# Stick-breaking attention: causal mask as a table on VectorE instead of mask products on TensorE, and softplus in four ScalarE passes

## The reference, cut to what matters

```python
z = jnp.einsum('bqhd,bkhd->bhqk', q, k).astype(jnp.float32) * (HEAD_DIM ** -0.5)
z = z + b_sb.astype(jnp.float32)[None, :, None, None]
mask = k_pos[None, :] < q_pos[:, None]
log_keep = jnp.where(mask, jax.nn.log_sigmoid(-z), 0.0)
after = lax.cumsum(log_keep, axis=3, reverse=True) - log_keep
a = jnp.where(mask, jnp.exp(jax.nn.log_sigmoid(z) + after), 0.0)
return jnp.einsum('bhqk,bkhd->bqhd', a.astype(v.dtype), v)
```

## Time and profile before

| | |
|---|---|
| median of three runs | 875.83 us (872.63, 875.83, 875.88) |
| the profiled execution's own time | 872.5 us |
| its span in the trace | 870.7 us |
| PE busy | 825.4 us |
| DVE, ACT, POOL busy | 526.9, 348.9, 376.9 us |
| granted TensorE clock, mean | 0.989 |

### The profile page before, as it was taken

The page is one execution under the profiler, slowest core; times in us unless marked ns, Lnnn a source line. Parts: engine busy times, 40 slices in busy tenths (PEclk is TensorE's granted clock), DMA queues, the critical chain, the costliest instruction groups (busy, mean ns, idle before and its releaser), DMA issues.

```text
span 870.7 us, 15500 instructions
## 1 busy us (share of the span) xinstructions
PE 825.4 (95%) x4267; PEld 488.4 (56%) x4267; DVE 526.9 (61%) x691; ACT 348.9 (40%) x682; POOL 376.9 (43%) x186
## 2 busy tenths in 40 slices
PE   0899989999999999999999999999999999899996
PEld 0455756555667565565765655658555555344442
DVE  2554678676584767737857768287686774223334
ACT  6311057574112575811136666211565741111222
POOL 0006782653677355525865455268446430100000
PEclk9989999999999999999999999999999999999998
DMA  8997685576788866657888675687986757373101
GB/s 320 331 309 254 219 268 168 170 226 207 234 253 270 276 208 215 222 172 252 270 271 261 223 244 177 200 256 252 282 249 212 238 185 302 106 236 100 71 24 51
DMA packets 129221, 191.25 MB, mean 220 GB/s; under 512 B 9817, under 2 KB 50822, under 8 KB 129121
## 3 DMA queue, kind: packets, MB, share of 16 engines
q1 hardware_dynamic: 97920, 174.38, 60.9%
q10 hardware_dynamic: 31200, 15.73, 6.4%
HBM read 181.58 MB, written 8.51 MB: 218 GB/s over the span
## 4 chain that ended last, share of the span: by engine, by line
PE 88%; DVE 3%; issue 2%; SPq 2%; DMA 2%; ACT 1%; POOL 1%; POOLq 0%; DVEq 0%; ACTq 0%
PE ps L1144 83%; PE ps L1300 4%; DMA pages<-in_page_table_dram 1%; PE ps L1185 1%; SPq L319 1%; POOL prod L539 1%; DMA hT<-in_w_out_dram 1%; DVE xy L851 1%; DVE ps L1024 0%; DMA ring<-in_cache_v_dram 0%; PE ps L1327 0%; SPq L359 0%; SPq L351 0%; DVE zc L1030 0%; ACT gcb L572 0%
## 5 line engine op out<-in xcount | busy, mean ns | idle before, releaser
L1144 PE MATMUL ps<-hT,wsl 128*128 128x344 f32 x1344 | 425.3, 458 | 3.5 <-issue 3.5
L539 POOL TENSOR_TENSOR prod<-ring,qb 128x1024 f32<-128x1024 f32 x128 | 313.2, 2470 | 220.3 <-DMA ring<-in_cache_k_dram 93.9
L1144 PEld LDWEIGHTS ps<-hT,wsl 128*128 128x128 f32 x1344 | 241.6, 190 | 156.7 <-issue 43.0
L1000 DVE TENSOR_REDUCE zd<-prod 128x16 f32<-128x1024 f32 x128 | 154.1, 1213 | 37.1 <-POOL prod L539 35.9
L1010 DVE TENSOR_SCALAR zc<-ps,bsb 128x512 f32<-128x512 f32 (+3 forms) x96 | 55.5, 613 | 70.3 <-PE ps L1144 68.9
L1144 PE MATMUL ps<-ring,apad 128*8 128x512 f32 (+1 forms) x608 | 82.9, 626 | 2.5 <-DMA ring<-in_cache_v_dram 2.2
L572 ACT ACTIVATE av<-ps 128x512 f32<-128x512 f32 (+3 forms) x96 | 46.7, 487 | 86.2 <-PE ps L1300 85.4
L1144 PE MATMUL ps<-hT,xy 128*128 128x512 f32 x160 | 72.1, 594 | 0.5 <-DMA hT<-in_w_out_dram 0.5
L1024 DVE TENSOR_TENSOR_SCAN ps<-rise,ps 128x512 f32<-128x512 f32 (+3 forms) x64 | 65.6, 1025 | 9.8 <-ACT ps L572 8.7
L1144 PEld LDWEIGHTS ps<-wsl,hT 128*128 128x128 f32 (+1 forms) x576 | 63.5, 181 | 6.2 <-ACT vN L572 2.6
L1144 PE MATMUL ps<-wsl,hT 128*128 128x128 f32 (+1 forms) x576 | 66.5, 275 | 0.0
(11 more groups left out here) (210 smaller groups left out, 662.6 us busy)
## 6 DMA issues: line engine op xcount, KB each, us to landing
ring<-in_cache_k_dram SPq DMA_DIRECT2D x256, 256.0 KB, 3.0
ring<-in_cache_v_dram SPq DMA_DIRECT2D x256, 256.0 KB, 3.0
wsl<-in_w_in_dram ACTq DMA_DIRECT2D x30, 512.0 KB, 5.7
ring<-in_w_ada_dram SPq DMA_DIRECT2D x6, 2048.0 KB, 11.3
xy<-in_x_prompt_dram SPq DMA_DIRECT2D x2, 2048.0 KB, 10.4
out_dram<-oT SPq DMA_DIRECT2D x8, 512.0 KB, 4.0
ring<-in_x_prompt_dram SPq DMA_DIRECT2D x8, 512.0 KB, 6.5
hT<-in_w_out_dram SPq DMA_DIRECT2D x5, 512.0 KB, 5.6
```

What stands on the lines that cost most here:

```text
L539: pool.tensor_tensor(prod[:, p % 2].rearrange("p (j c) -> p j c", j=2), kring[:, p % 4], qb[:, p // 16].unsqueeze(1).to_broadcast([P, 2, H ...
L1000: v.tensor_reduce(zd[:, t // 16, :, r:r + 2], prod[:, t % 2].rearrange("p (j h d) -> p h j d", j=2, h=NH), AX_X, ALU.add)\
L1144: return nc.tensor.matmul(out, l, r, start=start, stop=stop, skip_group_check=True)
```

## The change

The mask moves from PE to DVE. A table `seen` (128 x 512, float32) is made once: in its last 128 columns it holds -2^100 where key is not before query and +2^100 elsewhere. The clamp of a diagonal unit becomes minimum(z + bias, table); that of the others adds the bias alone. The clamp at 40 is gone, so softplus is made as relu(zc) + ln(1 + exp(-abs(zc))), in four ACT passes: Abs, Exp, Ln, Relu. The scan reads `rise` unshifted, and the carry is a copy.

```diff
-            pool.memset(unseen[:, :], HIDE).then_inc(pool_const, 1)
-            pool.memset(ident_b[:, :], 0.0).then_inc(pool_const, 1)
+            pool.memset(seen[:, :], HIDE).then_inc(pool_const, 1)
...
+            pool.affine_select(out=seen[:, :], in_=seen[:, :], compare_op=ALU.is_ge, fill=-HIDE, base=P - QC,
+                               pattern=[[1, QC]], channel_multiplier=-1).then_inc(pool_const, 1)
...
-                        run(rise[:, u % 2, lo:QC], ps[:, Z + u % 3, 0:QC - lo], ACT.Relu, rise_ready,
-                            bias=bsh[:, bass.ds(2 * g + head, 1)])
                         z = sp[:, u % 2, lo:QC]
-                        run(z, zc[:, u % 3, lo:QC], ACT.Exp, exp_done)
+                        run(z, zc[:, u % 3, lo:QC], ACT.Abs, abs_done)
+                        act.wait_ge(abs_done, NU * g + u + 1)
+                        run(z, z, ACT.Exp, exp_done, scale=-1.0)
                         act.wait_ge(exp_done, NU * g + u + 1)
                         run(ps[:, Z + u % 3, 0:QC - lo], z, ACT.Ln, ln_done, bias=1.0)
+                        run(rise[:, u % 2, lo:QC], zc[:, u % 3, lo:QC], ACT.Relu, rise_ready)
...
-                v.tensor_scalar(zc[:, u % 3, lo:QC], ps[:, Z + u % 3, 0:QC - lo],
-                                bsb[:, bass.ds(2 * g + h, 1)], CLAMP, ALU.add, ALU.min).then_inc(zc_ready, 1)
+                t, b0, nb, _ = UNITS[u]
+                bias = bsb[:, bass.ds(2 * g + h, 1)]
+                if b0 + nb - 1 == t:
+                    v.scalar_tensor_tensor(zc[:, u % 3, lo:QC], ps[:, Z + u % 3, 0:QC - lo], bias, seen[:, lo:QC],
+                                           ALU.add, ALU.min).then_inc(zc_ready, 1)
+                else:
+                    v.tensor_scalar(zc[:, u % 3, lo:QC], ps[:, Z + u % 3, 0:QC - lo], bias, None, ALU.add)\
+                        .then_inc(zc_ready, 1)
...
-                v.tensor_tensor_scan(back(sums), back(rise[:, par_, lo + 1:QC + 1]), back(sums),
+                v.tensor_tensor_scan(back(sums), back(rise[:, par_, lo:QC]), back(sums),
                                      start, ALU.add, ALU.add).then_inc(scan_done, 1)
...
-                    v.tensor_scalar(carry[:, h:h + 1], sums[:, 0:1], rise[:, par_, 0:1], None, ALU.add)\
+                    v.tensor_copy(carry[:, h:h + 1], sums[:, 0:1])\
                         .then_inc(carry_ready, 1)
...
-                    diagonal = b0 + nb - 1 == t
-                    if diagonal:
-                        for h in range(2):
-                            mm(ps[:, Z + (u + h) % 3, P * (nb - 1):P * nb], unseen[:, :], ident_b[:, :], True, False)
                     for h in range(2):
                         rows_ = slice(HD * h, HD * (h + 1))
-                        z = mm(ps[:, Z + (u + h) % 3, 0:P * nb], qT[rows_, P * t:P * (t + 1)],
-                               kT[rows_, P * b0:P * (b0 + nb)], not diagonal, True)
-                        z.then_inc(z_full, 1)
+                        mm(ps[:, Z + (u + h) % 3, 0:P * nb], qT[rows_, P * t:P * (t + 1)],
+                           kT[rows_, P * b0:P * (b0 + nb)], True, True).then_inc(z_full, 1)
```

More of the change, by code:

```diff
@@ L48 @@
 EPS = 1e-6
-CLAMP = 40.0
 HIDE = -2.0 ** 100
@@ L57 @@
 SAMPLE_AT = OUT_UNITS - 3
-POOL_CONSTS = 9
+POOL_CONSTS = 7
 SLOTS = 32
@@ L140, in stick_breaking_mixer @@
         zc = sb("zc", [P, 3, QC])
-        rise = sb("rise", [P, 2, QC + 1])
+        rise = sb("rise", [P, 2, QC])
         carry = sb("carry", [P, 2])
-        bsh = sb("bsh", [P, NH])
         last2 = sb("last2", [P, 2])
@@ L163, in stick_breaking_mixer @@
         nones = sb("nones", [P, P], F32R)
-        unseen = sb("unseen", [P, P], BF16)
-        ident_b = sb("ident_b", [P, P], BF16)
+        seen = sb("seen", [P, QC])
         ones = sb("ones", [P, P])
@@ L213, in stick_breaking_mixer @@
         q_out = sem("q_out"); q_full = [sem(f"q_full{k}") for k in range(2)]
-        z_full = sem("z_full"); zc_ready = sem("zc_ready"); exp_done = sem("exp_done")
+        z_full = sem("z_full"); zc_ready = sem("zc_ready"); abs_done = sem("abs_done"); exp_done = sem("exp_done")
         ln_done = sem("ln_done"); rise_ready = sem("rise_ready")
@@ L487, in _ @@
             pool.memset(half[:, :], -0.5).then_inc(pool_const, 1)
-            pool.memset(unseen[:, :], HIDE).then_inc(pool_const, 1)
-            pool.memset(ident_b[:, :], 0.0).then_inc(pool_const, 1)
-            pool.wait_ge(pool_const, 5)
+            pool.memset(seen[:, :], HIDE).then_inc(pool_const, 1)
+            pool.wait_ge(pool_const, 4)
             pool.affine_select(out=ident[:, :], in_=ident[:, :], compare_op=ALU.not_equal, fill=1.0, base=0,
@@ L820, in _ @@
             v.memset(keep[:, :, :], 1.0).then_inc(dve_const, 1)
-            v.memset(rise[:, :, QC:QC + 1], 0.0).then_inc(dve_const, 1)
             v.memset(naught[:, :], 0.0).then_inc(dve_const, 1)
-            v.wait_ge(dve_const, 9)
+            v.wait_ge(dve_const, 8)
             v.memset(keep[:, :, 0:1], 0.0).then_inc(dve_const, 1)
@@ L829, in _ @@
             v.tensor_copy(nones[:, :], minus1).then_inc(dve_const, 1)
-            v.wait_ge(dve_const, 13)
+            v.wait_ge(dve_const, 12)
             v.wait_ge(c_act, 3)
@@ L875, in _ @@
                                     ALU.mult, ALU.add).then_inc(h_ready, 1)
-            link(v.tensor_scalar(bsh[:, :], bsb[:, :], -CLAMP, None, ALU.add))
             PRO = links[0]
@@ L1156, in _ @@
             last.then_inc(par_full, 1)
-            pe.wait_ge(dve_const, 13)
+            pe.wait_ge(dve_const, 12)
             pe.wait_ge(cT_copied, 1)
```

## The result

The changed kernel takes **877.17 us** (median of 11 runs, 876.12 to 879.40). The kernel before, run beside it, takes 874.74 us (11 runs, 872.48 to 875.88). The ratio is 1.0034 [1.0022, 1.0046]: 2.4 to 3 us slower, where 6.8 us were forecast. The direction was right, the size was not. 877.2 lies inside the recorded range of 875.5 to 888, near its lower end, and within 0.5% of before, an outcome that had a chance of 0.21.

The account below looks back on a forecast made before the run. PE was taken as the bound, busy 95% of the span, other engines costing only when late for it. Masks -3.6 us plus turn waits 10.4 gave +6.8 on 875.83, 882.6 us; range 875.5 to 888 for 8 in 10.

Parts of the forecast that it names:

- Masks off PE, 3.6 us: Ahead of the 32 diagonal score pairs, removing 64 mask products saves PE 0.112 us a pair, 3.6 us.
- The table clamp, the carry copy, POOL's set-up: On DVE and POOL, the clamp reading a table (751 ns against 747), the copy and the set-up cost nothing.
- rival D: On DVE, the table clamp fights POOL for SBUF, taking about 1.26 us for 512 columns; about 893 us, chance 0.04.
- The passes, +0.59 us a wide unit with the scan behind relu: On ACT, four passes take 2.44 us instead of 1.83 in a unit of 512 columns, with relu last.
- the seven turns: PE's transposes of units 6, 8, 12, 16, 18, 20, 22 in each group, forecast to wait for the longer chain.
- The mean of the seven is 0.20, so the reserve is 0.20 - 0.05 = 0.15: At seven turns a group, 0.15 us is free from subtraction end to weight load, so 7 x (0.59 - 0.15) = 3.1 us.
- That the narrow units 0, 2, 4, 10 and 14 would not wait: In groups 2 to 4 their turns feel nothing: the reserve exceeds their pass or DVE is late anyway.
- the forecast's 10.4 us: Added PE waits at the turns of all four groups, 3.1 + 3.1 + 4.2 us; bounds 6.2 and 12.4.
- B, the other side: At the turns, the chain has unseen room, so only the masks count: 872.2 us, chance 0.12.
- C: ACT's queue becomes the bound and av delays the next score pair too; about 890 us, chance 0.08.
- E: TensorE's clock falls to its lower level in places of the attention stretches; about 916 us, chance 0.02.
- The base: The time of the kernel before that the sum was added to: median of three runs, 875.83 us.

Follow-up runs that it names:

- numbers4_after: The changed kernel with SyncE reading four page numbers at once where two pairs follow each other; 874.69 us, ratio 0.9999 to before.
- numbers4_before: The kernel before with SyncE reading four page numbers at once where two pairs follow each other; 872.67 us, ratio 0.9977.
- The fifth pass: The kernel before with softplus in four passes and a plain-addition clamp, masks kept on PE, plus an ACT copy ahead of Relu; 895.45 us, ratio 1.0224.
- the pair with the shorter reading of page numbers: The kernel before and the changed kernel, each with SyncE reading four page numbers at once; 872.67 and 874.69 us.
- numbers4_masks: The kernel before with the table clamp, no mask products and three passes, plus SyncE reading four page numbers at once; 871.02 us, ratio 0.9952.
- masks_only: The kernel before with the table in DVE's clamp and no mask products, its three passes kept; 872.03 us, ratio 0.9969.
- passes_only: The kernel before with softplus in four passes and the clamp a plain addition, mask products kept on PE; 881.09 us, ratio 1.0072.
- before_again: The kernel before, unchanged, executed once more for a second trace; 875.44 us, span 873.7.
- turn_later: The changed kernel with one more projection product ahead of the turns of even units; 874.27 us, ratio to before 1.0005.

## Why the prediction was right in direction and wrong in size

**Masks off PE, 3.6 us: right.** 28 pairs give 0.112 us each. The four that open a group give 0.421 - 0.203 = 0.218, which I had set equal to the others: 4.0 us, or 63 ns for a mask. The 81 ns of the Trainium skill ("TensorE: Matmul & The Clock Gate", section Back-to-back issue gap) would be 5.2 us. The traces differ from it both ways, 56 ns a mask inside a group and 109 at the four openings, and their sum decides for 4.0.

**The table clamp, the carry copy, POOL's set-up: right.** 746 ns; rival D is refuted.

**The passes, +0.59 us a wide unit with the scan behind relu: right.** By unit 16's rows 2.47 us against 2.44; the chain from score to subtraction grew by 0.63 us as the mean of the seven turns (slack used and wait added), where 0.59 was forecast.

**"The mean of the seven is 0.20, so the reserve is 0.20 - 0.05 = 0.15": this step failed.** I took the reserve from the subtraction's end to the weight load. What PE needs is the matmul, and the load stands 0.29 us ahead of it. By starts of matmuls, unit 16 of group 2 had 344.88 - 344.31 = 0.57 us, unit 18 had 0.24 and not 0.05. Less the 0.06 at which a waiting matmul follows the subtraction, the seven have 3.0 us in hand in group 2 as in group 3, 0.42 each, and 3.4 in groups 1 and 4. So 7 x 0.63 - 3.0 = 1.4 us a group, and 1.0 in group 4. With the queue out of the way (numbers4_after less numbers4_before) the traces show 1.5, 1.5 and 1.0 in groups 2, 3 and 4, and 1.7 in group 1, at its units 2, 6 and 8: 5.7 us together instead of 10.4. A row of the prediction said so already: unit 18's load already waited 0.20 us, and yet PE was busy 101.0 of 101 us. The fifth pass, with nothing left in hand, cost what the formula says.

With that term corrected, and in the pair with the shorter reading of page numbers, where no scan waits for decode keys, the sum is -4.0 + 5.7 = +1.7 us, or +2.9 with the 1.2 us of the late second matmuls (22 more). The medians differ by 874.69 - 872.67 = +2.0. In the runs of the change itself they differ by +2.4. The agreement is of the total alone: the halves both fall short. numbers4_masks gains 1.7 us on numbers4_before where the sum has 4.0, and numbers4_after loses 3.7 on numbers4_masks where it has 5.8 to 7.0. With 12 runs each such a difference is good to about 1.7 us.

The recorded range has two figures that no run shows: the masks at 5.2 us, in its lower end, where the traces give 4.0, and at 2, in its upper end.

**That the narrow units 0, 2, 4, 10 and 14 would not wait, "or DVE is late anyway": incomplete.** In the pair of traces units 2, 4 and 8 of groups 3 and 4 carry 4.7 us of waits, 4.4 beyond what unit 8 waits in group 2; the first trace of before has none. They make the 10.9 us of that pair look like the forecast's 10.4. They are not the passes': masks_only has them too, passes_only has not, and the second trace of before has 2.5 us of them. Nor are they all extra time, for the seams are shorter where they occur: by 2.7 us in the changed kernel, 1.7 in masks_only and 1.6 in before_again, against waits of 4.4, 4.0 and 2.5 us. As I read it, not shown by a run of its own, the decode stream (SyncE's queue, then POOL, then DVE) keeps its own pace through the seam, and how PE's lateness divides between seam and unit 2 differs from run to run. My view of one execution had all of it at the seam.

**B, the other side, was the nearer rival**: its mechanism (a reserve unseen at the load) was the true one, with 0.42 us a turn, less than a pass of 0.63. For the masks to win it would have needed 0.63 - 0.14 = 0.49 or more, since 4.0 us over 28 turns are 0.14 each. C did not occur in the changed kernel. Its sign, score pairs that wait behind av, appears in turn_later, where the turn and not ACT's queue makes av late. E occurred in a small form, and not through the change: inside attention and at the seams products at half clock appear behind some waits of PE of 1.7 us and more, with the kernel before's order as well (numbers4_before from 118.4 us, at the end of 2.46 us of idle, and from 398.3, behind 2.21). The changed kernel's trace stays at full clock from 54.6 to 754.3 us; both kernels' traces have half clock around 50 and 750 us. The Trainium skill's rule that short idles make the clock swing ("TensorE: Matmul & The Clock Gate", section A second HAM failure mode: psum-queue depth-cycling) did not come true at the changed kernel's turns: in its trace products stay 0.289 us apart behind every one of their waits, the longest of which is 2.6 us.

The base was 1 us high as well: three runs gave 875.8, the later sets 874.5 to 875.0.

**Still open:** masks_only wins 2.6 us of 4.0 and numbers4_masks over numbers4_before 1.7. Between 58 and 740 us their traces hold episodes at half clock (1.4 and 2.8 us) that the first trace of before has not, but numbers4_before has 2.8 too; I can't say from one trace each how often they come. Why PE waits at the seam is not settled either; the rows give "issue" as the reason.

**The version that beats both kernels** is numbers4_masks: masks as a table in the clamp, three passes, four page numbers at once; 871.0 us, 0.3 to 0.7% under before. It hides masked columns from the exponential, but relu(z - 40) sees their scores, which is sound only while these stay under 40. If that can't be promised, numbers4_after (874.7) costs what the kernel before does and has neither cap nor mask products.

## What to carry to other kernels

Read the reserve of a matmul that waits for data at the matmul's start, not at its weight load; a load's idle bracket is a warning, PE's own bracket is a cost. A first extra pass on a chain may be cheap and the second dear: add one to find out how much is left. Where a sum meets the measured total, see whether its halves meet theirs. Before a small difference is placed in stages, take a second trace of the same kernel, because engines that run their own stream trade waits between stages.

## What the runs showed of the hardware

- A VectorE pass that reads and writes SBUF only (max with 0, 512 columns) takes 0.42 us alone, and up to 2.6 us when it starts beside a POOL operation; in the same trace the clamp of 512 columns, which reads PSUM, takes 740 to 753 ns each time.
- One pair of pages on SyncE costs 2.26 us of its queue, of which the two DMA issues are 0.85. With four numbers read at once the second pair follows the first by 1.11 us and two pairs take 3.7 us (numbers4_masks, 386.2 to 390.0 us).
- After idle times of PE of 1.7 to 2.8 us three to six products run at half the clock in some executions, at once or about 1 us later (0.51 over 562 to 565 us in numbers4_masks), 0.9 to 1.7 us for each episode, and in others not at all (the changed kernel's first turn waited 2.6 us without it).
- A turn whose weight load starts late, together with its first matmul, has its second matmul 0.165 us behind the first, and 0.109 where the load ran ahead.
